# Full-array products in a recurrence, and reordered ends of two expert stages

## The chip, the cores and the metric

One NeuronCore of a Trainium2 chip runs the whole program. The metric is the device time of one execution in microseconds (us), the median of several. The kernel before takes 2805.59 us (three runs, 2804.86 to 2808.12). TensorE does the matrix products, VectorE, ScalarE and GpSimd the elementwise work, and SyncE issues most DMAs. In the rows they are PE (PEld is its weight loads), DVE, ACT, POOL and SP.

## The reference

The reference has two blocks over 1024 tokens of width 1024, all in float32. The first block mixes windowed attention, a gated linear recurrence and an RWKV-7 recurrence. The second has two layers, each a mixer followed by a mixture of 64 experts.

Two parts matter here. The RWKV-7 recurrence, with 4 heads of 64, is

```
sa = state @ (-kk_t)
state = state * w_t + sa * b_t + v_t * k_t      # per head, 64 x 64
y_t = state @ r_t
```

The experts and the end of the network are

```
hh = silu(xb @ w_gate[e]) * (xb @ w_up[e]);  ys = hh @ w_down[e]
h = h + gate_0 * ys_0 + gate_1 * ys_1            # two experts per token
out = rmsnorm(h, final_norm_g)                   # after the last layer
```

## The kernel before

`chunks` computes the recurrence in chunks of 64 tokens, 16 in all. Each chunk needs the inverse of a unit triangular 64 x 64 matrix per head. Four heads lie in two tiles `t` of two 64-row halves. The helper `all_of` issues four 64 x 64 products, one for each tile and half, and these go to the four quarters of the array. Two chunks are in work at once, an even one (`e`) and an odd one (`o`), in the buffers `X[c]` and `Y[c]` of PSUM. The order on every engine is written out by hand in the loops over `ROUNDS`, 8 rounds of two chunks. `cross` begins a chunk with five calls of `all_of`, thus 20 products. `step(J, n)`, for n of 0 to 3, squares the matrix power, multiplies the inverse by it, and adds the old inverse with `all_of(..., eye, ...)`, a product with the 64 x 64 identity `idh`. ScalarE copies each result out (`step_copy`) before the next step may start.

`experts` runs 32 pairs of experts in each layer. SP streams gate, up and down weights into a ring of three slots. For pair `p` PE does the gate products, then `last_product(p - 1)` (the down products of the pair before), the up products, the transposes of the next pair's rows and of the hidden values. POOL gathers rows and scatters results to `ys` in DRAM. After the scatter of the last but one pair it executes a `drain`, and then issues the last scatter. `after.start` loads what the next stage needs, and `after.rows_in` loads rows of `ys` once both scatters' semaphores are in.

After layer 0 the next stage is `combine_and_latents` (class `LatentLoads`), after layer 1 it is `combine_out` (class `FinalLoads`). For each 128-token tile `combine_out` forms the sum of the residual and two gated rows in two VectorE instructions (`gathered_sum`, lines 3554 and 3555), ScalarE squares it, and VectorE scales it (3987, 3988) before SP stores it.

Of the kernel before, what the change touches and what calls it, by code (L numbers as in the profile page):

```python
# [8 lines left out]
ALU = mybir.AluOpType  # L9
# [137 lines left out]
def front(nc, D, proj, values, kkb, bb, dlt, wc, vec, win, ck):  # L147
# [5 lines left out]
    with Phase(nc, "fr") as ph:  # L153
# [73 lines left out]
        with nc.Block() as block:  # L227
# [365 lines left out]
            def _(dve):  # L593
# [160 lines left out]
                V.tensor_tensor(rr, rr, aa[:], ALU.mult)  # L754
                V.scalar_tensor_tensor(out=kkb[:], in0=kkb[:], scalar=-1.0, in1=lw[:], op0=ALU.mult, op1=ALU.mult)
# [190 lines left out]
def chunks(nc, D, proj, kkb, bb, bonus, wc, vec, ck, next_loads):  # L946
# [13 lines left out]
    with Phase(nc, "rwc") as ph:  # L960
        z, masks, idh = ck.z, ck.masks, ck.idh
# [25 lines left out]
        eps_set = ph.sem("eps_set")  # L987

# [16 lines left out]
        with nc.Block() as block:  # L1005
# [49 lines left out]
            def _(dve):  # L1055
                V = nc.vector
                V.memset(eps[:], GN_EPS).then_inc(eps_set, 1)

# [34 lines left out]
                def rows_add(J):  # L1093
                    c, j = place(J)
                    if 0 <= J < NCH:
                        V.tensor_tensor(gr[:, c, :, 1], blocks(Y[c], 1), proj[:, R_T:R_T + TL, columns(J)], ALU.add
                                        ).then_inc(gr_out[c], 1)
# [136 lines left out]
            def _(pe):  # L1234
# [10 lines left out]

                def cross(J):
                    c, j = place(J)
                    if J < NCH:
                        if j:
                            pe.wait_ge(y_out[c], j)  # L1250
                        r, k = (proj[:, f:f + TL, columns(J)] for f in (R_T, CK_T))
                        a, b = (x[:, :, columns(J)] for x in (kkb, bb))
                        all_of(blocks(X[c], 0), b, r, 0, 1)
                        all_of(blocks(X[c], 1), b, a, 0, 1)
                        all_of(blocks(X[c], 2), k, r, 0, 1)
                        all_of(blocks(X[c], 3), k, a, 0, 1)
                        all_of(blocks(X[c], 4), a, b, 0, 1).then_inc(crossed[c], 1)

                def turn_in(J):
                    c, j = place(J)  # L1260
                    if J < NCH:
                        if j:
                            pe.wait_ge(z_out[c], j)
                        val, k = (proj[:, f:f + TL, columns(J)] for f in (CV_T, CK_T))
                        a, b = (x[:, :, columns(J)] for x in (kkb, bb))
# [27 lines left out]
                def step(J, n):  # L1293
                    c, j = place(J)
                    if 0 <= J < NCH:
# [5 lines left out]
                        if n < SQ - 2:  # L1301
                            all_of(blocks(X[c], 1, 2), pw0, flat(steps[:, c, :, 1:3]), at, 1, True, False)
                            all_of(blocks(X[c], 2), eye, steps[:, c, :, 2], at, 1, False, True)
                            last = all_of(blocks(X[c], 0), pw1, pw0, at, 1)
                        elif n == SQ - 2:
                            all_of(blocks(X[c], 1), pw0, steps[:, c, :, 2], at, 1, True, False)
                            all_of(blocks(X[c], 1), eye, steps[:, c, :, 2], at, 1, False, True)
# [43 lines left out]

                for i in range(ROUNDS + 1):
# [419 lines left out]
def first(nc, D, proj, next_loads):  # L1772

    with Phase(nc, "V") as pv:
# [11 lines left out]
        chunks(nc, D, proj, kkb, bb, bonus, wc, vec, ck, next_loads)  # L1786
# [1325 lines left out]
def expert_loads(nc, D, layer):  # L3112
# [12 lines left out]
    return gate_in, up_in, down  # L3125


def experts(nc, D, layer, tokens, keep, spill, gate, gu_slots, d_slots, xe, g_loaded, u_loaded, d_loaded, x_loaded, after, within):
# [4 lines left out]
    gate_in, up_in, down = expert_loads(nc, D, layer)  # L3133
    with Phase(nc, "ex", within) as ph:
# [39 lines left out]
        y_stored = [ph.sem(f"y{b}_stored") for b in range(2)]  # L3174
        hn_dram, y_rows = D["hn"], D["ys"].rearrange("t (c d) -> (t c) d", c=2)
# [150 lines left out]
        with nc.Block() as block:  # L3326

            @block.sync
            def _(sp):
                for p in range(RING, PAIRS_M):  # L3330
# [8 lines left out]
                    for n in range(2):  # L3339
                        down(sp, d_slots[r][n], p + n * PAIRS_M, d_loaded[r])  # L3340
# [4 lines left out]
                after.start(sp)  # L3345
                with sp.If(0 < count):
# [14 lines left out]
                for t in range(after.NBUF):  # L3361
                    after.rows_in(sp, t)

            @block.gpsimd
            def _(pool):
# [23 lines left out]
                for p in range(PAIRS_M - 2, PAIRS_M):  # L3389
                    pool.wait_ge(m["y_out"], 2 * (p + 1))  # L3390
                    scatter(p)
                    if p < PAIRS_M - 1:
                        pool.drain()
                for b in range(2):
# [15 lines left out]
            def _(pe):  # L3410
# [29 lines left out]
                last_product(PAIRS_M - 1)  # L3440
# [23 lines left out]
            def _(act):  # L3464
# [12 lines left out]
                for p in range(PAIRS_M):  # L3477
                    act.wait_ge(m["g_done"], p + 1)
                    silu(p % 2).then_inc(m["silu_done"], 1)
                    if p >= 1:  # L3480
# [26 lines left out]
            def _(dve):  # L3507
# [41 lines left out]
                after.scale_second(nc, dve)  # L3549
# [649 lines left out]
```

## Time and profile before

| | |
|---|---|
| median of three runs | 2805.59 us |
| the profiled execution's own time | 2810.32 us |
| its span | 2808.6 us |
| PE, share of the span | 2464.8 us, 88% |
| DVE | 1072.5 us, 38% |
| ACT | 538.4 us, 19% |
| POOL | 343.6 us, 12% |
| mean granted TensorE clock | 0.95 of full |

The span is the time from the first to the last instruction of the profiled execution. Busy shares are averages over all stages, and each stage has its own limit. The recurrence lies from 384 to 517 us, layer 0's experts end near 1610 us, layer 1's near 2761 us, and `combine_out` runs from there to the end.

### The profile page before, as it was taken

Reading aid. Unit: us, or ns where it says so; the run is one execution under the profiler, and the core shown is the slowest. Engines: PE = TensorE matmul, PEld = TensorE weight load, DVE = VectorE, ACT = ScalarE, POOL = GpSimd, SP = SyncE. Lnnn points to the kernel's source line nnn. Section 1 sums busy time; section 2 is a strip of 40 time slices with the busy share of each in tenths; the row PEclk is TensorE's granted clock in tenths of the full one; section 3 lists DMA queues with packets and bytes.
Section 4 is the critical chain, followed back from the end, with each engine's and each line's share of the span. In section 5 each row is a group of like instructions: output and inputs, shape, how many; then the busy total and the mean of one; then the engine's idle time right before and its main releaser. Section 6 shows DMA issues by size and latency. Waiting matters only on the chain. (4 is left out here: it accounts for less than half of the span.)

```text
span 2808.6 us, 40012 instructions
## 1 busy us (share of the span) xinstructions
PE 2464.8 (88%) x16506; PEld 1581.8 (56%) x16506; DVE 1072.5 (38%) x2183; ACT 538.4 (19%) x1220; POOL 343.6 (12%) x362
## 2 busy tenths in 40 slices
PE   9999988898999898988878789999999988877882
PEld 5444567547888555555545455666674555544551
DVE  3472654666455643211111154444545521111114
ACT  1311454210000011111111131322331111111112
POOL 3321002400000211111111000000004011111110
PEclk9999999998999999999999989999999999999896
DMA  3111010231113237999999970000103499999997
GB/s 116 36 40 53 1 47 5 78 112 37 40 45 117 98 105 280 409 420 419 420 420 420 375 284 16 17 24 8 61 35 144 175 387 419 420 420 420 420 420 300
DMA packets 111033, 566.11 MB, mean 202 GB/s; under 512 B 22000, under 2 KB 22160, under 8 KB 59376
## 3 DMA queue, kind: packets, MB, share of 16 engines
q1 hardware_dynamic: 85808, 506.87, 44.9%
q0 software_dynamic: 20144, 38.79, 3.7%
q10 hardware_dynamic: 4896, 17.83, 1.6%
q8 instruction: 135, 2.21, 0.3%
q14 instruction: 50, 0.41, 0.0%
HBM read 529.06 MB, written 65.01 MB: 212 GB/s over the span
## 5 line engine op out<-in xcount | busy, mean ns | idle before, releaser
L3205 PE MATMUL ex__h_ps<-all__arena,ex__xT 128*64 128x256 f32 x3392 | 529.9, 418 | 166.5 <-DMA all__arena<-in_w_gate 105.6
L3205 PEld LDWEIGHTS ex__h_ps<-all__arena,ex__xT 128*64 128x64 f32 x3392 | 339.6, 151 | 336.4 <-issue 221.5
L3248 DVE COPY ex__ysb<-ex__y_ps 128x512 f32<-128x512 f32 x64 | 44.3, 692 | 630.6 <-PE ex__y_ps L3225 630.2
L3205 PE MATMUL ex__h_ps<-mo__wx,ex__xT 128*64 128x256 f32 x704 | 180.3, 415 | 0.0
L3369 POOL DMA_INDIRECT b__rows<-s_hn,mo__queue x60 | 60.6, 1010 | 760.5 <-PE ex__x_ps L3198 760.5
L3225 PE MATMUL ex__y_ps<-b__w,ex__hT 128*64 128x512 f32 x672 | 152.2, 592 | 0.9 <-ACT ex__hT L3242 0.9
L2535 PE MATMUL cm__acc<-all__arena,cw__w 128*128 128x260 f32 x576 | 136.0, 386 | 2.3 <-PEq L84 2.3
L2535 PE MATMUL cm__acc<-all__arena,cm__sums 128*128 128x260 f32 x576 | 135.0, 384 | 0.0
L2535 PEld LDWEIGHTS cm__acc<-all__arena,cw__w 128*128 128x128 f32 x576 | 110.4, 192 | 19.8 <-issue 2.7
L2535 PEld LDWEIGHTS cm__acc<-all__arena,cm__sums 128*128 128x128 f32 x576 | 110.2, 191 | 17.2
L2921 PE MATMUL hd__o<-all__arena 128*128 128x128 f32 x704 | 98.4, 283 | 15.3 <-ACT all__arena L2990 15.3
L3236 ACT ACTIVATE ex__sg<-ex__h_ps 128x256 f32<-128x256 f32 x64 | 24.5, 383 | 419.3 <-PE ex__h_ps L3205 419.3
L2921 PEld LDWEIGHTS hd__o<-all__arena 128*128 128x128 f32 x704 | 85.5, 191 | 31.9 <-ACT all__arena L2990 25.5
L3205 PEld LDWEIGHTS ex__h_ps<-mo__wx,ex__xT 128*64 128x64 f32 x704 | 103.5, 150 | 0.0
L3239 DVE TENSOR_TENSOR ex__hs<-ex__sg,ex__h_ps 128x256 f32<-128x256 f32 x64 | 27.0, 421 | 186.6 <-PE ex__h_ps L3205 186.6
L3225 PEld LDWEIGHTS ex__y_ps<-b__w,ex__hT 128*64 128x64 f32 x672 | 54.0, 137 | 73.2 <-issue 67.5
L1956 POOL MEMSET mo__ident<- 128x128 f32 x2 | 0.4, 204 | 743.5 <-POOLq L84 743.5
L3230 ACT COPY ex__xT<-ex__x_ps 128x512 f32<-128x512 f32 x64 | 37.4, 585 | 275.6 <-PE ex__x_ps L3198 275.6
L2076 PE MATMUL pb__acc<-b__w,all__arena 128*128 128x512 f32 x192 | 87.9, 603 | 1.8 <-PEq L84 1.8
L374 PE MATMUL fr__acc<-X__xT,fr__w 128*128 128x512 f32 x192 | 87.0, 603 | 0.0
L3198 PE MATMUL ex__x_ps<-mo__ident,b__rows 128*128 128x128 f32 x512 | 75.7, 292 | 9.1 <-PEq L84 9.1
L3198 PEld LDWEIGHTS ex__x_ps<-mo__ident,b__rows 128*128 128x128 f32 x512 | 63.2, 195 | 34.5 <-issue 34.5
(534 smaller groups left out, 4194.9 us busy)
## 6 DMA issues: line engine op xcount, KB each, us to landing
all__arena<-in_w_gate SPq DMA_DIRECT2D x106, 1024.0 KB, 27.7
all__arena<-in_w_up SPq DMA_DIRECT2D x106, 1024.0 KB, 27.1
b__w<-in_w_down SPq DMA_DIRECT2D x84, 1024.0 KB, 27.4
all__arena<-in_w_down SPq DMA_DIRECT2D x22, 1024.0 KB
mo__wx<-in_w_gate SPq DMA_DIRECT2D x22, 1024.0 KB, 28.5
mo__wx<-in_w_up SPq DMA_DIRECT2D x22, 1024.0 KB
mo__wx<-in_w_down SPq DMA_DIRECT2D x22, 1024.0 KB
all__arena<-s_ys SPq DMA_DIRECT2D x16, 1024.0 KB, 8.9
```

Of the source, the lines that this page charges most:

```text
L374: last = mm(acc[:, bank], weight[:, k], moving(k), start=(first and k == 0), stop=(k == HKT - 1), skip_group_check=not first)
L2076: last = mm(acc[:, bank], weight[:, k], moving[:, k], start=(first and k == 0), stop=(last_here and k == HK - 1), skip_group_check=not first)
L2535: last = nc.tensor.matmul(bank(u, x), weight(k), moving(k, c), start=(k == 0), stop=(k == HK - 1))
L2921: last = mm(o_ps[:, h, 0:P], vv[:, s, h], pT[:, h, 4 * g + a], start=(g == 0 and a == 0), stop=(g == end and a == len(tiles_of(i)[g]) - 1))
L3198: last = nc.tensor.transpose(x_ps[:, k // 4, P * (k % 4):P * (k % 4) + P], xe[:, b, k::KT], ident[:])
L3205: last = nc.tensor.matmul(h_ps[half, c, DE * b:DE * b + DE], xT[:, b, k, half], slots[n][:, c, k], start=(k == 0), stop=(k == KT - 1))
L3225: last = nc.tensor.matmul(y_ps[half, c], hT[:, b, k, half], slots[n][:, k, 512 * c:512 * c + 512], start=(k == 0), stop=(k == 1))
L3230: return nc.scalar.copy(xT[:, b, 0:4].rearrange("p k q -> p (k q)"), x_ps[:, 0])
L3236: return nc.scalar.activation(sg[:, b], h_ps[:, 0, DE * b:DE * b + DE], ACT.Silu)
L3239: return nc.vector.tensor_tensor(hs[:, b], sg[:, b], h_ps[:, 1, DE * b:DE * b + DE], ALU.mult)
L3248: return nc.vector.tensor_copy(ysb[:, b, 512:], y_ps[:, 1])
L3369: g.indirect_dma_start(xe[:, p % 2], None, hn_dram[:, :], bass.IndirectOffsetOnAxis(ap=queue[:, 0, p:p + 1], axis=0), bounds_check=T - 1, ...
```

## The change

The changes in the recurrence are these. `front` now leaves `rr` in the tile `XB_T` and `-kk` in `R_T`, so that both are neighbours and one moving operand of 128 columns. `cross` then takes two calls of 128 columns and one of 64, thus 12 products. A new tile `swap` holds the identity with its halves exchanged. `kept` adds the old inverse by two products of the full 128 x 128 array, with `ident` and `swap` as weights, in place of four quarter products.

In `experts`, at the last pair, PE does `last_product(p - 1)` ahead of the gate products, and ACT its half of the copy ahead of `silu`. The last pair's down weights come in four loads, one for each row `k` and expert, with semaphores `d_ends`, and `down_half` computes in the order of `k`. A semaphore `scatter_sent` lets SP issue `after.middle`. `LatentLoads` loads `wk` there, and its residual tiles 1 and 2 between the rows of `ys`. `scale_second` moves from the experts' end into `combine_and_latents`, after `make(1)`. `FinalLoads` loads three residual tiles at first, two in `middle`, three later.

`combine_out` no longer reuses buffers: all eight tiles of rows have their own. For tiles 2, 4 and 6 PE forms the sum, with weights `ident` and `spread` (the identity times a gate's column, made by ACT), and ScalarE and VectorE read it from PSUM. The tiles are taken in the order of `TURNS`.

```diff
-                V.tensor_tensor(rr, rr, aa[:], ALU.mult)
-                V.scalar_tensor_tensor(out=kkb[:], in0=kkb[:], scalar=-1.0, in1=lw[:], op0=ALU.mult, op1=ALU.mult)
+                v(V.tensor_tensor(proj[:, XB_T:XB_T + TL], rr, aa[:], ALU.mult))
+                V.scalar_tensor_tensor(out=rr, in0=kkb[:], scalar=-1.0, in1=lw[:], op0=ALU.mult, op1=ALU.mult)
...
+                V.tensor_copy(swap[:, 0:HALF], ident[:, HALF:P]).then_inc(swap_made, 1)
+                V.tensor_copy(swap[:, HALF:P], ident[:, 0:HALF]).then_inc(swap_made, 1)
...
+                def kept(out, of):
+                    for t, weights in enumerate((ident, swap)):
+                        nc.tensor.matmul(out[:, t], weights[:], of[:, t], start=False, stop=True)
...
-                        r, k = (proj[:, f:f + TL, columns(J)] for f in (R_T, CK_T))
-                        a, b = (x[:, :, columns(J)] for x in (kkb, bb))
-                        all_of(blocks(X[c], 0), b, r, 0, 1)
-                        all_of(blocks(X[c], 1), b, a, 0, 1)
-                        all_of(blocks(X[c], 2), k, r, 0, 1)
-                        all_of(blocks(X[c], 3), k, a, 0, 1)
-                        all_of(blocks(X[c], 4), a, b, 0, 1).then_inc(crossed[c], 1)
+                        ra = proj[:, XB_T:R_T + TL, columns(J)].rearrange("p (f t) k -> p t f k", f=2)
+                        k, b = proj[:, CK_T:CK_T + TL, columns(J)], bb[:, :, columns(J)]
+                        all_of(X[c][:, :, 0:2 * HALF].rearrange("p t (f k) -> p t f k", f=2), b, ra, 0, 1)
+                        all_of(X[c][:, :, 2 * HALF:4 * HALF].rearrange("p t (f k) -> p t f k", f=2), k, ra, 0, 1)
+                        all_of(blocks(X[c], 4), ra[:, :, 1], b, 0, 1).then_inc(crossed[c], 1)
...
                             all_of(blocks(X[c], 1, 2), pw0, flat(steps[:, c, :, 1:3]), at, 1, True, False)
-                            all_of(blocks(X[c], 2), eye, steps[:, c, :, 2], at, 1, False, True)
+                            kept(blocks(X[c], 2), steps[:, c, :, 2])
...
+            return last
+
+        def down_half(b, slots, k):
+            for c in range(2):
+                for n in range(2):
+                    half = slice(CAP * n, CAP * n + CAP)
+                    last = nc.tensor.matmul(y_ps[half, c], hT[:, b, k, half], slots[n][:, k, 512 * c:512 * c + 512],
+                                            start=(k == 0), stop=(k == 1))
...
+                    if p < PAIRS_M - 1:
+                        for n in range(2):
+                            down(sp, d_slots[r][n], p + n * PAIRS_M, d_loaded[r])
+                    else:
+                        for k in range(2):
+                            for n in range(2):
+                                down_rows(sp, d_slots[r][n], p + n * PAIRS_M, k, d_ends[k])
...
                 after.start(sp)
+                sp.wait_ge(scatter_sent, 1)
+                after.middle(sp)
...
+                    end = p == PAIRS_M - 1
+                    if end:
+                        last_product(p - 1)
                     pe.wait_ge(m["xT_out"], 2 * (p + 1))
                     pe.wait_ge(g_loaded[p % RING], 32 * (p // RING + 1))
                     gate_products(p % 2, gu_slots[p % RING]).then_inc(m["g_done"], 1)
-                    if p >= 1:
+                    if p >= 1 and not end:
                         last_product(p - 1)
...
-                last_product(PAIRS_M - 1)
+                pe.wait_ge(m["hT_out"], PAIRS_M)
+                pe.wait_ge(m["y_out"], 2 * (PAIRS_M - 1))
+                for k in range(2):
+                    pe.wait_ge(d_ends[k], 32)
+                    last = down_half((PAIRS_M - 1) % 2, d_slots[(PAIRS_M - 1) % RING], k)
+                last.then_inc(m["y_done"], 1)
...
+    def middle(self, sp):
+        sp.dma_start(self.wk[:], self.D["w_dkv_t"]).then_inc(self.wk_loaded, 16)
+
+    def rows(self, sp):
+        for t in range(self.NBUF):
+            self.rows_in(sp, t)
+            if t + 1 < self.NBUF:
+                self.residual_in(sp, t + 1)
...
                 make(1)
+                pre.scale_second(nc, dve)
                 scale(1)
...
+        BY_PE = (2, 4, 6)
+        TURNS = (0, 1, 3, 2, 5, 4, 7, 6)
...
+                for t in range(NBUF, TT):
+                    if t > NBUF:
+                        pre.residual_in(sp, t)
+                    sp.dma_start(yb[t], D["ys"][P * t:P * t + P]).then_inc(y_loaded[t], 16)
...
+                        nc.tensor.matmul(acc[:, n, c], ident[:], hb[:, t, part_of], start=True, stop=False)
+                        for e in range(2):
+                            last = nc.tensor.matmul(acc[:, n, c], spread[:, n, e], yb[t][:, DM * e + 512 * c:DM * e + 512 * c + 512],
+                                                    start=False, stop=(e == 1))
...
+                make(0)
+                make(1)
+                scale(0)
+                make(3)
+                scale(1)
+                make(5)
+                scale(2)
+                scale(3)
+                make(7)
+                scale(4)
+                scale(5)
+                scale(6)
+                scale(7)
```

On PE, here is a piece of the recurrence's first round: before, from the odd chunk's `cross` to the even chunk's step 0 and the odd chunk's `square`.

```order
L1241 MATMUL rwc__x<-all__arena,V__bb 64x64 x4
L1241 MATMUL rwc__x<-V__kkb,V__bb 64x64 x4
L1241 MATMUL rwc__x<-all__arena 64x64 x4
L1241 MATMUL rwc__x<-V__kkb,all__arena 64x64 x4
L1241 MATMUL rwc__x<-V__bb,V__kkb 64x64 x4
L1241 MATMUL rwc__y<-rwc__big 64x64 x4
L1241 MATMUL rwc__x<-rwc__steps 64x128 x4
L1241 MATMUL rwc__x<-rwc__steps,V__idh 64x64 x4
L1241 MATMUL rwc__x<-rwc__steps 64x64 x4
L1241 MATMUL rwc__x<-rwc__big 64x64 x8
```

The same place on PE now:

```order
L1245 MATMUL rwc__x<-all__arena,V__bb 64x128 x4
L1245 MATMUL rwc__x<-all__arena 64x128 x4
L1245 MATMUL rwc__x<-V__bb,all__arena 64x64 x4
L1245 MATMUL rwc__y<-rwc__big 64x64 x4
L1245 MATMUL rwc__x<-rwc__steps 64x128 x4
L1253 MATMUL rwc__x<-rwc__steps,V__ident 128x64
L1253 MATMUL rwc__x<-rwc__steps,rwc__swap 128x64
L1245 MATMUL rwc__x<-rwc__steps 64x64 x4
L1245 MATMUL rwc__x<-rwc__big 64x64 x8
```

The 20 products of `cross` became 12, and the four quarter products with `idh` became two of the full array, with quarter products on either side of them. A row's shape is that of its output.

On SP, here are the loads at layer 1's end before, from the last pair's gate weights on (`ys` rows are those of the final stage):

```order
L3117 DMA all__arena<-in_w_gate 128x2048
L3117 DMA mo__wx<-in_w_gate 128x2048
L3120 DMA all__arena<-in_w_up 128x2048
L3120 DMA mo__wx<-in_w_up 128x2048
L3123 DMA b__w<-in_w_down 128x2048 x2
L3923 DMA all__arena<-s_h 128x1024 x8
L3924 DMA all__arena<-in_final_norm_g 128x1024
...
L3933 DMA all__arena<-s_ys 128x2048 x4
...
L3933 DMA all__arena<-s_ys 128x2048
L3960 DMA out<-all__arena 128x1024
L3933 DMA all__arena<-s_ys 128x2048
```

And now:

```order
L3125 DMA all__arena<-in_w_gate 128x2048
L3125 DMA mo__wx<-in_w_gate 128x2048
L3128 DMA all__arena<-in_w_up 128x2048
L3128 DMA mo__wx<-in_w_up 128x2048
L3134 DMA b__w<-in_w_down 128x1024 x4
L3972 DMA all__arena<-in_final_norm_g 128x1024
L3985 DMA all__arena<-s_h 128x1024 x5
...
L3991 DMA all__arena<-s_ys 128x2048 x4
...
L4028 DMA all__arena<-s_ys 128x2048
L3985 DMA all__arena<-s_h 128x1024
L4028 DMA all__arena<-s_ys 128x2048
```

Three residual loads moved behind the first five tiles of rows, and the stores of `out` moved behind all loads.

## Rows read from the trace of the kernel before

**Rows 1.** The chain of waits, layer 1's end: start us, us, what.

```profile
2714.22 28.23 DMA mo__wx<-in_w_gate
...
2742.59 3.67 PE ex__h_ps L3205 x32
2746.26 3.45 PE ex__y_ps L3225 x16
...
2752.24 8.47 issue
...
2761.46 4.05 DMA s_ys<-ex__ysb,mo__queue
...
2765.96 7.31 DMA all__arena<-s_ys
...
2773.37 1.30 DVE all__arena L3554
...
2802.65 1.29 DVE all__arena L3988
```

**Rows 2.** Groups of instructions, DVE, 2770 to 2808 us: count, busy us, mean ns.

```profile
L3555 DVE SCALAR_TENSOR_TENSOR all__arena<-all__arena,all__gate 128x1024 f32<-128x1024 f32 x8 | 10.3, 1285 | 0.3
L3988 DVE SCALAR_TENSOR_TENSOR all__arena<-all__arena,co__rs 128x1024 f32<-128x1024 f32 x8 | 10.3, 1285 | 0.3
...
L3987 DVE RECIPROCAL co__rs<-co__rt 128x1 f32<-128x1 f32 x8 | 1.3, 163 | 1.0
```

**Rows 3.** Busy time by stretch, line 1241: length, PE, PEld (counts), clock, DMA.

```profile
384.00:517.00 133.00, 109.51 (x4322) 98.69 (x4323) 0.98 0.08 28
```

**Rows 4.** DMA queues, 384 to 517 us: packets, MB, share of 16 engines.

```profile
q8 instruction: 34, 0.56, 1.8%
```

**Rows 5.** Waits, 384 to 517 us: who for whom, us in total, times, longest.

```profile
PE rwc__x L1241 <- issue: 14.6, 19, 1.8
...
PE rwc__y L1241 <- issue: 3.3, 5, 0.9
...
PEld rwc__x L1241 <- ACT rwc__steps L1181: 5.9, 21, 0.7
```

**Rows 6.** Timeline of PE, 434 to 453 us: start, us, [idle before].

```profile
443.60 0.21 PE L1241 MATMUL rwc__y<-V__idh,all__arena 64*64 64x64 f32 x1 [0.81 <-issue]
```

**Rows 7.** Timeline of PE, 441.2 to 442.3 us.

```profile
441.31 0.45 PE L1241 MATMUL rwc__x<-rwc__steps 64*64 64x128 f32 x8
441.58 0.29 PE L1241 MATMUL rwc__x<-rwc__steps,V__idh 64*64 64x64 f32 x8
...
442.03 0.29 PE L1241 MATMUL rwc__x<-rwc__steps,V__idh 64*64 64x64 f32 x8
442.14 0.30 PE L1241 MATMUL rwc__x<-rwc__steps 64*64 64x64 f32 x8
```

**Rows 8.** Timeline of PE's weight loads, 441 us, quarter array.

```profile
441.31 0.21 PEld L1241 LDWEIGHTS rwc__x<-rwc__steps 64*64 64x64 f32 x8 [0.29 <-ACT rwc__steps L1181]
```

**Rows 9.** Timelines of PE, 300 us, and PEld, 2739 us: changes of the array's tiling.

```profile
300.10 1.02 PE L838 MATMUL swa__f<-X__xT,all__arena 128*128 128x512 f32 x2
301.05 0.72 PE L804 MATMUL swa__s<-all__arena 64*128 64x128 f32 x8
...
2739.27 0.97 PEld L3198 LDWEIGHTS ex__x_ps<-mo__ident,b__rows 128*128 128x128 f32 x8 [0.39 <-issue]
```

**Rows 10.** Timelines of POOL, PE and DVE, layer 0's end.

```profile
1613.00 0.97 POOL L3374 DMA_INDIRECT s_ys<-ex__ysb,mo__queue  x1 [9.86 <-issue]
...
1592.01 0.66 PE L3205 MATMUL ex__h_ps<-all__arena,ex__xT 128*64 128x256 f32 x1 [4.24 <-DMA mo__wx<-in_w_gate]
...
1610.07 2.46 DVE L3600 TENSOR_SCALAR all__arena<-all__arena,fw__gains 128x320 f32<-128x320 f32 x8
1621.30 1.28 DVE L3554 SCALAR_TENSOR_TENSOR all__arena<-all__arena,all__gate 128x1024 f32<-128x1024 f32 x1 [8.78 <-DMA all__arena<-s_ys]
```

**Rows 11.** Busy time by stretch: length, PE, PEld, DVE, ACT, POOL, clock, DMA share, GB/s.

```profile
1580.00:1590.00 10.00, 7.77 (x56) 4.83 (x52) 1.80 (x3) 1.45 (x3) 0.97 (x1) 1.00 1.01 420
```

More of the change, by code:

```diff
@@ L1263, in turn_in @@
                             pe.wait_ge(z_out[c], j)
[L1264 to L1265 removed]
+                        a, val, k = (proj[:, f:f + TL, columns(J)] for f in (R_T, CV_T, CK_T))
+                        b = bb[:, :, columns(J)]
                         all_of(blocks(Y[c], 0), a, eye, 0, 1)
@@ L1306, in step @@
                             all_of(blocks(X[c], 1), pw0, steps[:, c, :, 2], at, 1, True, False)
-                            all_of(blocks(X[c], 1), eye, steps[:, c, :, 2], at, 1, False, True)
+                            kept(blocks(X[c], 1), steps[:, c, :, 2])
                             last = all_of(blocks(X[c], 0), pw1, pw0, at, 1)
@@ L3174, in experts @@
         y_stored = [ph.sem(f"y{b}_stored") for b in range(2)]
+        d_ends = [ph.sem(f"d_end{k}_loaded") for k in range(2)]
+        scatter_sent = ph.sem("scatter_sent")
         hn_dram, y_rows = D["hn"], D["ys"].rearrange("t (c d) -> (t c) d", c=2)
@@ L3360, in _ @@
                     sp.wait_ge(y_stored[b], 16 * (PAIRS_M // 2))
-                for t in range(after.NBUF):
-                    after.rows_in(sp, t)
+                after.rows(sp)
             @block.gpsimd
@@ L3477, in _ @@
                 for p in range(PAIRS_M):
+                    end = p == PAIRS_M - 1
+                    if end:
+                        y_half(p - 1)
                     act.wait_ge(m["g_done"], p + 1)
                     silu(p % 2).then_inc(m["silu_done"], 1)
-                    if p >= 1:
+                    if p >= 1 and not end:
                         y_half(p - 1)
@@ L3921, in start, with middle, rows, residual_in @@
     def start(self, sp):
-        for t in range(self.TT):
-            sp.dma_start(self.hb[:, t], self.h_in[P * t:P * t + P]).then_inc(self.h_loaded[t], 16)
         sp.dma_start(self.gb[:], self.D["final_norm_g_2"].partition_broadcast(P)).then_inc(self.g_loaded, 16)
+        for t in range(3):
+            self.residual_in(sp, t)
+    def middle(self, sp):
+        for t in range(3, 5):
+            self.residual_in(sp, t)
+    def rows(self, sp):
+        for t in range(self.NBUF):
+            self.rows_in(sp, t)
+    def residual_in(self, sp, t):
+        sp.dma_start(self.hb[:, t], self.h_in[P * t:P * t + P]).then_inc(self.h_loaded[t], 16)
     def scale_first(self, nc, act):
-        pass
-    def scale_second(self, nc, dve):
         pass
@@ new lines, in _ @@
+                for n, t in enumerate(TURNS):
+                    sp.wait_ge(scaled, n + 1)
+                    sp.dma_start(D["out"][P * t:P * t + P], ho[:, t]).then_inc(out_stored, 16)
+                sp.wait_ge(out_stored, 16 * TT)
+            @block.gpsimd
+            def _(pool):
+                make_identity(nc, pool, ident, const_done)
+                nc.gpsimd.memset(eps[:], NORM_EPS).then_inc(const_done, 1)
+            @block.tensor
+            def _(pe):
+                pe.wait_ge(const_done, 3)
+                for n, t in enumerate(BY_PE):
+                    pe.wait_ge(h_loaded[t], 16)
+                    pe.wait_ge(spread_done, 2 * (n + 1))
+                    pe.wait_ge(y_loaded[t], 16)
+                    for c in range(2):
+                        part_of = slice(512 * c, 512 * c + 512)
+                        nc.tensor.matmul(acc[:, n, c], ident[:], hb[:, t, part_of], start=True, stop=False)
+                        for e in range(2):
+                            last = nc.tensor.matmul(acc[:, n, c], spread[:, n, e], yb[t][:, DM * e + 512 * c:DM * e + 512 * c + 512],
+                                                    start=False, stop=(e == 1))
+                    last.then_inc(summed, 1)
@@ new lines, in _ @@
+                for n, t in enumerate(BY_PE):
+                    for e in range(2):
+                        nc.scalar.activation(spread[:, n, e], ident[:], ACT.Copy, scale=gate[:, t, e:e + 1]
+                                             ).then_inc(spread_done, 1)
+                nc.scalar.activation(rt[:, 1:2], eps[:], ACT.Sqrt)
+                for n, t in enumerate(TURNS):
+                    b = n % 2
+                    if t in BY_PE:
+                        act.wait_ge(summed, BY_PE.index(t) + 1)
+                    else:
+                        act.wait_ge(made, by_dve.index(t) + 1)
+                    if n >= 2:
+                        act.wait_ge(scaled, n - 1)
+                    nc.scalar.activation(sq[:], sums_of(t), ACT.Square, accum_out=ss[:, b:b + 1]).then_inc(squared, 1)
+                    act.wait_ge(squared, n + 1)
@@ L4049, in moe @@
         x_loaded = [ph.sem(f"x{b}_loaded") for b in range(2)]
-        gate_in, up_in, down = expert_loads(nc, D, layer)
+        gate_in, up_in, down, _ = expert_loads(nc, D, layer)
         gu = lambda tile: part(tile, 2, KT, DE)
```

92 lines of the change are left out of this document (42 added, 50 removed).

## The prediction

> **What bounds the kernel now.** I read the chain of waits first, then the stretches it passes through. At layer 1's end it shows a row of single causes [rows 1]: the last gate weights land at 2742.45 us, PE does gate products and then the down products of the pair before, GpSimd sits 8.47 us between its last two scatters, the last scatter lands, the first rows of `ys` land, and from there VectorE alone carries the chain to 2803.94. Layer 0 ends the same way [rows 10].
>
> The recurrence is 133 us in which PE is busy for 109.5 and DMA is nearly idle [rows 3]. The reader should look at the queue of instructions there: 34 packets with 0.56 MB, thus 16 KB each [rows 4]. `chunks` issues 136 products for each of 16 chunks, and every one appears as two weight loads and two matmuls, 8704 instructions in all (8645 are recorded, rows 3). 8704 over 34 packets is 256, so a packet is 256 instructions. PE's idle time has mostly no releaser, "issue": 14.6 and 3.3 us [rows 5], in gaps like the one of 0.81 us [rows 6]. 133 us over 34 packets is 3.9 us a packet. I read this as PE waiting for its own instructions: it uses up 256 in about 3 us and gets the next after 3.9. After these come short waits for ScalarE's copy of a step, 5.9 us [rows 5].
>
> **The recurrence, removed and added.** Four quarter products run side by side. With 64 columns they take 0.115 us (442.03 to 442.14 [rows 7]); with 128 columns 0.27 us after a wait, of which some 0.05 are the first weights, so 0.22 [rows 7].
>
> `cross`: five calls at 0.115 are 0.575 us; now twice 0.22 and once 0.115 are 0.555. That gains 0.02 x 16 = 0.3 us of PE, but 8 products, thus 32 instructions, a chunk. `kept` saves two products, 8 instructions, in each of four steps, 32 more. 64 x 16 = 1024 instructions are four packets. Were the stage bound by packets alone, it would take 30 x 3.9 = 117 us.
>
> The price of `kept` stands in no row, so I build it. Its weights are 128 columns wide. Eight such loads in a row take 0.97 us, 0.11 from one to the next [rows 9], against about 0.055 for a round of quarter loads (two rounds in 0.21, one lasting 0.13 [rows 8]). Two products need four loads, and only 64 columns stream behind each, half as long as its successor's load. That is 4 x 0.11 + 0.055 = 0.495 us. Second, the array's tiling changes before and after. In rows 9 two full-array matmuls start 0.43 apart, so the second starts at 300.53 and has streamed by 300.96; the first of the other tiling starts at 301.05. That is 0.09 us in which nothing streams, and the first weight load behind it is open too (counted above going in, 0.055 going out). Together 0.09 + 0.495 + 0.09 + 0.055 = 0.73 us, in place of 0.115: 0.61 us more. Four steps in 16 chunks are 64 calls, 39 us of PE.
>
> The Trainium skill, "TensorEngine Tiling (Array Packing)", section Tiling Modes, Key Properties, says that changing the tiling mode, not merely the tile, drains TensorE. By that rule the 0.09 us are paid twice in every call, as the trace has it between other stages; without it 64 x 0.18 = 11.5 us would fall away and the kernel would come out near 2797 us, which is inside the first rival below.
>
> What hides it: the instruction waits. PE without them needs some 133 - 22 = 111 us (17.9 in rows 5, and a few us in gaps of the weight loads, which I set at 4). Plus 39, less 0.3: 150. In the steps PE alternates between two chunks. With 0.61 more for each, ScalarE's copies are always ready, so their 5.9 us go: 144. A block that now has fewer slow steps will still meet its packet late, 2 us. So 146 us, **+13 us**. The packets (117) are then no longer late on the whole. Bounds: -16 (packets alone decide, `kept` is free) and +28 (all 39 is added, and only 11 of the waits go). I take 13, since each of its terms has a row. Nothing covers the stage: all later stages start after it. The two copies for `swap` (VectorE, 128 x 64) and the moved outputs of `front` cost under 0.5 us.
>
> **Layer 0's end.** PE waits 4.24 us for gate weights until 1592.01 [rows 10]. The down products (3.45 us, as rows 1) now fit into this gap, from about 1588.5. But the up weights, 2.1 MB at 420 GB/s [rows 11], land 5 us after the gate ones, near 1597, so the up products start 3.5 us earlier than before and not more. The hidden copy and down products follow, and the last down weights (another 5 us, 1602) are just there. So the last results leave PE 3.5 us earlier. GpSimd's scatter at 1613.00 was late through its drain (9.86 us idle); the scatter before it moves ahead by over 8 us, so the drain is over, and the last scatter follows its data by 0.8 us in place of 2.9. Gain 5.6 us. Against it: `wk` (1.3 MB, 3.1 us) is now in the queue ahead of the rows and beside the scatter. I take off 1.1. The eight `scale_second` instructions (2.46 us) now stand on VectorE after `make(1)`, where it waited about 2 us for ScalarE; PE is the engine behind and has work. **-4.5 us**, bounds -5.6 and -1.
>
> **Layer 1's end.** PE waited only 1.9 us for the gate weights, so the down products move ahead, but products in all end 1.0 us earlier. The drain again: 1.6 us. The last scatter 2.6 us earlier; two residual loads (1 MB) now run beside it, which I price at 0.4. `combine_out`: before, VectorE takes 33.4 us, from 2770.5 (one sum and its wait ahead of 2773.37) to 2803.94, eight times two sums of 1.28, a reciprocal and a scaling of 1.285 and gaps [rows 1, 2]. Three tiles' sums leave it: 25 us of work. But then the loads bound it: after the first rows, 7 tiles of 1.05 MB and 3 residuals of 0.52 are 8.9 MB, 21.2 us at 420 GB/s; tile 7's sum and four scalings (2.6 + 4 x 1.5 with PSUM sources) end at 29.8. Gain 3.6. PE's six products for a tile are 12 matmuls at 0.43 [rows 9], 5.2 us at 2.4 GHz and 10.3 at 1.2 GHz; after idling it starts slowly (the first gate matmul of rows 10 lasts 0.66 us). Tile 6 is ready in time at the higher and 1 us late at the lower. **-5.8 us**, bounds -8 and -2.
>
> **Sum.** 13 - 4.5 - 5.8 = +2.7 us. Against its own time (span 2808.6, 2810.32 us in all) the profiled execution would become 2813.0. The median of the runs lies 4.7 below that, so 2805.6 + 2.7 = 2808 us. A measurement of this kernel tells differences over about 0.2%, 5.6 us; this is none.
>
> **Rivals.**
> Cheap full-array products: the loads are pulled ahead or the drain overlaps, and the packets decide. For it: PE idles 22 us today, and 1024 instructions go. Against: the gap of 0.09 and the 0.11 between loads. Stage 117 to 135 us, kernel 2779 to 2797, say 2789.
> Dear ones (slower): the stalls for packets do not give way, since where steps are dense the packets were not late and elsewhere they still are. It decides once more than 30 of the 39 us remain; then +23 in the stage, 2818 us. For it: the gap of rows 6 lies in a run of products that read no step. Against: there is a packet every 3.9 us, and each 256 instructions now hold two `kept`.
> The ends give nothing: the scatter is held by the new loads and rows land no earlier, or the final stage stays as long through PE at 1.2 GHz. Half of the gain: 2813 us. Against: the drain's 8.47 us in the chain.
>
> **Chances.** Forecast 0.48 (its own range 2801 to 2814), cheap 0.28, dear 0.16, ends 0.08. Faster by over 0.2%: 0.28 + 0.48 x 0.12 = 0.34. Slower: 0.16 + 0.06 and 0.15 of the forecast's 0.48 = 0.29. The same: 0.37. The range 2785 to 2819 leaves out the ends of both outer cases.
>
> **What would show it.** In the profile after: the recurrence at 146 us with 30 packets, "issue" on PE under 8 us, and about 0.6 us between the starts of the first full-array product and the next quarter product. A stretch of 120 us would refute the price of `kept`. GpSimd's last scatter 0.8 us behind VectorE's copy at both ends, and VectorE waiting for `ys` of tile 7. If the stage's idle time stayed at 18 us with `kept` in it, the reading of packets would be wrong.

## The result, and the profile after

The changed kernel takes 2818.86 us (median of 6 runs, 2815.07 to 2819.79), the kernel before, run beside it, 2806.86 us (2803.83 to 2808.87). The ratio is 1.0034, with a 95% interval of 1.0024 to 1.0044: slower by 9.5 us, 6.7 to 12.3. The two medians by themselves lie 12.0 us apart and the two profiled executions 8.9; this text goes by the ratio. The forecast was +2.7 us, 2808, and its own range ended at 2814. The range over all cases, 2785 to 2819, just holds the 2818.86, but only through the rival "dear ones" (2818), and the mechanism of that rival is not the one that acted. That the number lies there is luck.

A time is only the sum. What to read is when each stage begins in the two profiled executions (spans 2808.6 and 2817.5 us); the difference can only grow or shrink where something was changed, or where two executions of the same code differ. These are worked out from the records of each stage's tiles ("gate weights" is the start of the pair's first gate product; the recurrence is counted from the start of its first to the start of its last instruction):

| point in the program | before | after | difference |
|---|---|---|---|
| recurrence: first to last instruction | 137.6 | 149.4 | +11.8 |
| layer 0, experts begin | 1110.8 | 1121.5 | +10.7 |
| layer 0, gate weights of the pair before the two last | 1558.8 | 1570.3 | +11.5 |
| layer 0, last copy of results | 1609.37 | 1617.55 | +8.2 |
| layer 0, last scatter issued | 1613.00 | 1619.04 | +6.0 |
| layer 0, it has landed, rows of `ys` issued | 1615.98 | 1625.43 | +9.5 |
| attention's head stage begins | 1731.2 | 1741.8 | +10.6 |
| layer 1, gate weights, middle of the stream | 2512.4 | 2522.9 | +10.6 |
| layer 1, last copy of results | 2758.47 | 2769.56 | +11.1 |
| layer 1, last scatter issued | 2761.46 | 2771.04 | +9.6 |
| layer 1, landed, rows issued | 2765.59 | 2776.97 | +11.4 |
| first sum of the final stage | 2770.53 | 2782.40 | +11.9 |
| last scaling ends | 2803.9 | 2812.9 | +9.0 |

**The recurrence.** First what answers to [rows 3]: length of the window, busy us (and count) of PE, PEld, DVE, ACT and POOL, then the granted clock, DMA's share and GB/s.

```profile
384.00:532.00 148.00, 140.68 (x3840) 121.90 (x3840) 57.06 (x228) 65.86 (x177) 27.03 (x61) 0.98 0.07 25
```

PE now is busy for 140.7 of 148 us, where it was for 109.5 of 133. The instruction queue in the same stretch, answering to [rows 4]:

```profile
q8 instruction: 30, 0.49, 1.3%
```

And the waits of PE and of its weight loads, answering to [rows 5]: for what, us in total, times, the longest.

```profile
PE rwc__x L1245 <- ACT rwc__steps L1185: 3.0, 8, 0.4
PE rwc__y L1245 <- DVE rwc__yn L1138: 2.3, 2, 1.8
PEld rwc__x L1253 <- issue: 8.4, 48, 0.4
```

"issue" is gone from PE's matmuls. The 8.4 us on the weight loads of line 1253 are inside the full-array products. One such call (timeline of PE; a float32 product shows as two matmuls): six of the eight matmuls of four quarter products, which run side by side, then the two full-array products, then quarter products again.

```profile
459.69 0.39 PE L1245 MATMUL rwc__x<-rwc__steps 64*64 64x128 f32 x6
460.01 0.43 PE L1253 MATMUL rwc__x<-rwc__steps,V__ident 128*128 128x64 f32 x2
460.28 0.39 PE L1253 MATMUL rwc__x<-rwc__steps,rwc__swap 128*128 128x64 f32 x2
460.59 0.34 PE L1245 MATMUL rwc__x<-rwc__steps 64*64 64x64 f32 x8
```

In the records behind these rows the last quarter matmul starts at 459.81 and the next one behind the call at 460.59, 0.79 us later. In 48 of the 64 calls it is 0.79, made of 0.20, 0.16, twice 0.112, and 0.205 (in the other 16 it is 0.74); less the 0.056 that lie between two matmuls anyway, a call takes 0.73 us, the price that the prediction built.

**Layer 0's end.** VectorE, GpSimd and the DMA issues in after (start, us, what ended the idle time before), answering to [rows 10]:

```profile
1617.55 0.69 DVE L3269 COPY ex__ysb<-ex__y_ps 128x512 f32<-128x512 f32 x1 [4.79 <-PE ex__y_ps L3246]
1630.81 1.28 DVE L3592 SCALAR_TENSOR_TENSOR all__arena<-all__arena,all__gate 128x1024 f32<-128x1024 f32 x1 [12.57 <-DMA all__arena<-s_ys]
```
```profile
1619.04 0.98 POOL L3401 DMA_INDIRECT s_ys<-ex__ysb,mo__queue  x1 [11.16 <-DVE ex__ysb L3269]
```
```profile
1618.85 0.33 SPq L3626 DMA_DIRECT2D all__arena<-in_w_dkv_t  x1
1625.43 0.33 SPq L3654 DMA_DIRECT2D all__arena<-s_ys  x1
```

The reader should see three things. The last scatter now waits for VectorE's copy and follows its end by 0.8 us; the drain is no longer in the way. But by these records SP issues the load of `wk` 0.2 us ahead of it: `sem_inc` stands behind the scatter in the program and yet counted before the scatter's recorded start. And the rows of `ys` leave 6.4 us after the scatter, where before it was 3.0. What the DMA queues moved in the two halves of that time (q1 carries SP's loads, q0 the scatter; packets, MB, share of 16 engines), first from 1619 to 1622 us, then from 1622 to 1625.5:

```profile
q1 hardware_dynamic: 64, 0.66, 69.4%
```
```profile
q1 hardware_dynamic: 80, 0.66, 51.3%
q0 software_dynamic: 144, 0.30, 22.1%
```

The 1.3 MB of `wk` go first. In the first half not one packet of the scatter ends; all 144 are in the second. By the single DMA records its first packet starts at 1623.84, when 1.12 of the 1.31 MB have moved. Small as it is, 0.3 MB, it stands behind nearly the whole load.

**Layer 1's end.** PE's gate products of pair 30, before and after (timeline of PE):

```profile
2727.09 5.36 PE L3205 MATMUL ex__h_ps<-all__arena,ex__xT 128*64 128x256 f32 x32 [3.10 <-DMA all__arena<-in_w_gate]
```
```profile
2738.11 6.63 PE L3218 MATMUL ex__h_ps<-all__arena,ex__xT 128*64 128x256 f32 x32 [5.22 <-DMA all__arena<-in_w_gate]
```

It had idled for 5.2 in place of 3.1 us, and the same 32 products took 1.3 us more; the granted clock was lower around them, 0.57 against 0.76, so more of them ran at 1.2 GHz, the lower of the clock's two levels. These are the windows of before and of after, with the clock third from the end:

```profile
2726.00:2733.00 7.00, 5.91 (x36) 4.18 (x38) 0.00 (x0) 0.38 (x1) 0.00 (x0) 0.76 1.01 423
```
```profile
2737.00:2745.00 8.00, 6.88 (x35) 4.32 (x37) 0.00 (x0) 0.22 (x1) 0.00 (x0) 0.57 1.01 421
```

From there PE's work is the limit. The 1.0 us that the reordered down products save is thus lost before it begins. Nothing that PE does ahead of pair 31 was changed, and the idle time before the gate products of pairs 27 to 30 goes 1.9, 4.3, 3.1, 3.1 us in before and 3.1, 4.3, 2.0, 5.2 in after. As far as these records show, this loss is one of the two executions, not of the change. Then GpSimd and SP:

```profile
2758.91 0.98 POOL L3401 DMA_INDIRECT s_ys<-ex__ysb,mo__queue  x1 [8.17 <-DVE ex__ysb L3269]
2771.04 0.98 POOL L3401 DMA_INDIRECT s_ys<-ex__ysb,mo__queue  x1 [11.16 <-DVE ex__ysb L3269]
```
```profile
2745.13 26.53 SPq L3985 DMA_DIRECT2D all__arena<-s_h  x5
2776.97 1.98 SPq L3991 DMA_DIRECT2D all__arena<-s_ys  x4
```

Again 0.8 us from the copy to the scatter, and 5.9 us from there to the rows, where it was 4.1. The 4.1 were themselves unusual: of nine profiled executions with this end unchanged, seven show 3.0 us here and one other 4.1. Of the two residual loads one left 0.2 us ahead of the scatter, the other 0.2 us behind it. These are the last pieces of the chain of waits in after, answering to the end of [rows 1]:

```profile
2782.94 21.14 DMA co__own_rows<-s_ys
2804.18 1.30 DVE co__ho L3592
2805.50 1.30 DVE co__ho L3593
...
2811.61 1.28 DVE co__ho L4090
```

The final stage has become a stream of loads: tile 7 lands 21.1 us after its issue and 21.8 us after the first rows (2782.26 to 2804.08), for which the prediction had 21.2. From the first sum to the last scaling it takes 30.5 us, 33.4 before.

### The profile page after: what moved, and what is told of

It reads as the page before. It is cut to its first block and busy times, and to the rows that moved or that the text cites. A ratio compares the mean times of both kernels' runs of the same rounds, so it can differ in the third digit from the quotient of the medians.

```text
span 2817.5 us, 39067 instructions
## 1 busy us (share of the span) xinstructions
PE 2513.5 (89%) x16030; PEld 1607.7 (57%) x16030; DVE 1065.5 (38%) x2178; ACT 541.1 (19%) x1226; POOL 345.8 (12%) x365
## 5 line engine op out<-in xcount | busy, mean ns | idle before, releaser
L3238 PE MATMUL ex__y_ps<-b__w,ex__hT 128*64 128x512 f32 x640 | 144.8, 592 | 0.0
## 6 DMA issues: line engine op xcount, KB each, us to landing
all__arena<-in_w_gate SPq DMA_DIRECT2D x106, 1024.0 KB, 27.8
all__arena<-in_w_down SPq DMA_DIRECT2D x22, 1024.0 KB, 27.4
```

## Experiments

Each ran on a chip beside the kernel before; a difference is (ratio - 1) x that median, with its interval. "Stage" is the recurrence from its first to its last instruction. A first thing the runs show: four profiled executions with the same recurrence as before had stages of 137.6, 135.1, 136.1 and 134.4 us, 135.8 in the mean. The one on which the prediction rests was the longest.

**The two halves of the change.** Recurrence alone (`front`, `chunks` as in the change, the rest as before):

> The kernel before with the recurrence's part of the change alone (12 products in cross, the old inverse by full-array products), both experts' ends and the final stage as before. Theory A: the recurrence costs what it costs in the changed kernel (137.6 -> 149.4 us from its first to its last instruction), and the ends gave back only 2 us of it: the kernel is 11 us slower than before (9 to 13). Rival B (the ends themselves gained about what was forecast, and the recurrence costs more than its own stage shows): 16 us or more slower.

Measured: +14.3 us (10.4 to 18.3), median 2823.53; stage 150.1 us, 14.3 over the mean of before. The ends alone:

> The kernel before with the experts' ends and the final stage of the change alone, the recurrence as before. Theory A: 2 us faster (0 to 4), since in both layers the last scatter leaves 2 to 5 us earlier but lands 2 to 3.4 us later, beside the loads now sent with it. Rival B, the forecast: 10 us faster.

Measured: -2.0 us (-4.5 to +0.6), median 2807.69. B is refuted in its half on the ends: they give a fifth of what was forecast. For the recurrence alone A's 11 (9 to 13) was too low and B wanted 16 or more; the interval holds both. The stage's own 14.3 us are the whole 14.3, so nothing is lost outside it, and A's mechanism holds: A had measured from the longest stage of before. The cost is near the +13 of the forecast. The last scatters took 6.6 and 6.3 us to land.

**The two parts of the recurrence.** Twelve products, but in each step

```
-                            kept(blocks(X[c], 2), steps[:, c, :, 2])
+                            all_of(blocks(X[c], 2), eye, steps[:, c, :, 2], at, 1, False, True)
```

> The kernel before with 12 products in place of 20 in cross, the old inverse still added by quarter products. TensorE's own work changes by 0.3 us, but 512 of its instructions go, 2 of 34 packets. Theory A (before is bound by the arrival of instruction packets, 3.9 us each): the recurrence is 8 us shorter (6 to 12), the kernel as much faster. Rival C (the waits in before have another cause): within 1 us of before.

Measured: -5.6 us (-8.1 to -2.8), stage 129.9 us, 5.9 under the mean; the last run below, with the same recurrence, has 129.8. C is excluded; A has the sign, and its 8 (6 to 12) was a little too much. The other way round, `kept` with the twenty products:

> The kernel before with the old inverse added by two full-array products in each step, cross with its 20 products. 64 calls at 0.61 us are 39 us of TensorE more, and 2 packets fewer. Theory A (either the packets or the work is late, and here the work is): about 12 us slower in the recurrence (11 to 15), thus like the run with both parts of the recurrence. Rival D (the waits for packets stay and the work is added to them): 16 to 25 us slower.

Measured: +19.1 us (15.2 to 23.0), stage 153.3 us, 17.5 over the mean. A's 11 to 15 are missed, and both figures lie in D's 16 to 25. But D's mechanism is not there. The packets and the waits that nothing releases, of this run:

```profile
q8 instruction: 32, 0.52, 1.3%
```
```profile
PE rwc__x L1245 <- issue: 1.1, 3, 0.5
PE rwc__y L1245 <- issue: 0.5, 1, 0.5
```

The waits did give way (14.6 and 3.3 us in [rows 5]). What A lacked was in part the mean: it reckoned 22 us of waits in a stage that is 2 us shorter on average. The number alone would have misled, as it does for the whole change.

**What a call of `kept` is made of.** Behind its two products two more, with zero weights:

```
+                    for t in range(2):
+                        nc.tensor.matmul(out[:, t], nought[:], of[:, t], start=False, stop=True)
```

> The kernel before with the recurrence's part of the change, and in each of the 64 calls two more full-array products, whose weights are zero and which add nothing. They stand behind the first two, so the array's tiling changes no more often. Theory A (two full-array products are four weight loads of 0.11 to 0.13 us each, the rest of a call's 0.73 us is the change of tiling before and after): 28 to 33 us slower than the run with the recurrence alone. Rival F (most of a call's price is the change of tiling, and more products behind it cost 0.055 us each): 7 us slower.

Measured: +44.6 us (40.4 to 49.1), so 30 more than the recurrence alone; 30 / 64 is 0.47 us for two products, and in the records 0.83 us lie between the first and last matmul of a call in place of 0.38. Theory A, and F's 7 us is refuted: two products cost 0.45 us, four loads of 0.112. Of 0.73 us the remaining 0.28 go with the two changes of tiling, 0.14 each in the mean. This is a remainder; no run changed the tiling without the products.

**Are the gaps the packets'?** I counted matmuls from the start of the stage to each place where two starts lie over 0.28 us apart and PE waited for no semaphore. In before the first are at 267, 395, 522, 649, 775, 903, 1156, 1282, 1410, that is 267 and steps of 127 matmuls, each with its weight load: 254 instructions and one or two waits, 256. There are 27 such gaps, all on this grid, with 22.8 us above the usual 0.056. With 12 products there are 21 gaps and 14.0 us; with `kept` alone 8 and 3.5; in the run with the whole recurrence part 3 and 1.0. The DMA records say the same from the other side: in before, PE resumes 1.20 to 1.57 us after the end of an instruction packet at every one of the 27 gaps, while only 8% of all its matmuls start in that distance from a packet. The packets start 3.3 to 4.5 us apart there, 3.8 in the mean. So the gaps are waits for packets. To weigh the packets by a test I added instructions. First semaphore counts, 8 behind each of four steps:

```
+                        if n < SQ - 1:
+                            for _ in range(8):
+                                pe.sem_inc(counted, 1)
```

> The kernel before with 32 instructions more for TensorE in each of 16 chunks (8 behind each of four steps), which only add one to a semaphore that nobody reads: 512 instructions, two packets, as many as one of the recurrence's two parts takes away. Theory A (a packet of 256 instructions comes every 3.9 us, and before waits for it): the recurrence is 8 us longer in the sum, plus what these instructions cost by themselves, which the next run shows. Rival C (the gaps have another cause): longer only by what the next run shows.

> The kernel before with the recurrence's part of the change and the same 512 instructions. Here TensorE needs 149 us for its work and the packets would come in 32 x 3.9 = 125 us, so they are early. Theory A: longer than the recurrence alone only by what the instructions cost by themselves, 0 to 5 us, and at least 5 us less than they cost in the last run. Rival C: the same cost in both.

Measured: +42 us (37 to 47) and +26 us (21 to 30); stages 179.5 and 163.4 us. So the same 512 counts cost 43.7 us over the mean of before and 13.3 us over the recurrence alone. The sign is A's, the size of neither theory, and as a weighing of packets this test failed. A count is not cheap: they stand 0.15 us apart in the records, so eight keep PE's queue for 1.2 us. And in the first of the two runs the clock fell, which it did not in the second (columns as in after's window above; two windows of the first run, then one of the second):

```profile
386.00:470.00 84.00, 63.02 (x2053) 57.22 (x2047) 24.67 (x92) 31.13 (x81) 10.70 (x25) 0.83 0.11 40
470.00:560.00 90.00, 70.79 (x2247) 64.72 (x2243) 30.78 (x123) 34.27 (x96) 14.99 (x34) 0.79 0.01 4
```
```profile
386.00:470.00 84.00, 80.83 (x2052) 68.45 (x2044) 29.32 (x112) 34.99 (x92) 13.69 (x31) 0.98 0.11 39
```

The second attempt added narrow products in `cross`:

```
+                        for _ in range(4):
+                            all_of(X[c][:, :, 7 * HALF:7 * HALF + 8], b, b[:, :, 0:8], 0, 1)
```

> The kernel before with 16 more quarter products in each of 16 chunks (4 rounds of 4, only 8 columns wide, into a part of PSUM that nobody reads): 1024 instructions for TensorE, 4 packets, as many as the change takes away. By themselves they take at most what 64-column rounds take, 0.115 us each, so up to 7 us in all; the next run shows it. Theory A (a packet every 3.9 us, and before waits for it): the recurrence 12 to 20 us longer. Rival C (the gaps have another cause): as much longer as in the next run, up to 7 us.

> The kernel before with the recurrence's part of the change and the same 1024 instructions. It then needs 34 packets, 133 us, and TensorE has 149 us of work. Theory A: longer than the recurrence alone by the products' own time, 3 to 8 us, and by 7 us or more less than in the last run. Rival C: the same cost in both.

Measured: +14.6 us (9.5 to 19.4) and +27.8 us (23 to 32.6); stages 148.5 and 159.4 us. By the stages they cost 12.7 us over the mean of before, and 9.3 us over the recurrence alone, where packets are early; by the times 14.6 and 13.5 us, which are closer still. One gap of the first run, and its packets:

```profile
457.63 0.27 PE L1241 MATMUL rwc__x<-V__kkb,all__arena 64*64 64x64 f32 x2 [0.80 <-issue]
```
```profile
q8 instruction: 38, 0.62, 1.7%
```

Here the gaps are on nearly the same grid (267, 395, 649, 777, 903, 1031, ...) though other instructions stand there, all 30 of them end 1.2 to 1.5 us after a packet's end, and 38 packets by 3.9 us are 148.2. But the products' own price was 0.145 us a round, over my 0.115, and the two costs differ by 3 us by the stages and 1 us by the times, where A wanted 7 and C none; a stage varies by 3 us from one execution to the next. So this pair does not tell A from C. That the gaps are waits for packets is shown by the records. How much shorter the stage would be with all of them early is not: 12 products took 2 packets and 6 us, with 0.03 us a chunk of own work.

**What holds the last scatter up.** The ends again, but with `wk` and the two residual tiles issued in `start`, behind the last weights:

```
-                sp.wait_ge(scatter_sent, 1)
-                after.middle(sp)
```

> The run with the ends alone, but the loads that were issued between the last scatter and the rows of `ys` (wk in layer 0, two residual tiles in layer 1) are issued before it, behind the last weights, as in the kernel before. Theory A (these loads hold the last scatter up: it landed 6.4 us after its issue in layer 0 in place of 3.0, 5.9 in place of 4.1 in layer 1): both last scatters land in 3 to 4.2 us again; 5 us faster than the run with the ends alone, about 7 us faster than before. Rival E (the landing is longer for another reason, such as the rows of the scatter before it, which now leave closer to it): the landings stay at 6 us, no gain over the ends alone.

Measured: -9.8 us (-13.5 to -6.5), median 2797.58, and the two landings 3.0 and 3.5 us. GpSimd and SP in layer 0:

```profile
1606.23 0.97 POOL L3390 DMA_INDIRECT s_ys<-ex__ysb,mo__queue  x1 [11.34 <-DVE ex__ysb L3260]
```
```profile
1609.22 0.33 SPq L3640 DMA_DIRECT2D all__arena<-s_ys  x1
```

E is refuted: the scatter before the last stands as close as in the ends alone (12.3 and 12.4 us), only the load beside it is gone. In time the ends now give what the prediction gave them, 9.8 for 10.3, and more than A's 7; in the traces 2.7 us from layer 0's first expert to the head stage and 5.1 from layer 1's first expert to the last scaling. With the ends unchanged these two stretches themselves vary by 2 us between four executions (619.1 to 621.3 and 542.5 to 544.5 us). One step further:

```
-                pre.scale_second(nc, dve)
+                after.scale_second(nc, dve)
...
-        for t in range(5):
+        for t in range(self.TT):
             self.residual_in(sp, t)
```

> As the last, and moreover the eight scalings of wk stand in the experts' end again, and all eight residual tiles of layer 1 are loaded before its last scatter, so that the rows of `ys` are alone in the queue behind it. Expected: 1 us from the scalings, since VectorE no longer does 2.46 us of them between the second and third tile; and 2 to 3 us from the final stage, whose last tile waits for 1.5 MB less (3.7 us at 420 GB/s). In all 3 us faster than the last, 10 us faster than before (6 to 12). Rival: the residual tiles delay the last scatter or the last weights by as much, no gain.

Measured: -9.8 us (-13.2 to -6.5), median 2796.95, no gain over the last. In layer 1, GpSimd, SP and VectorE:

```profile
2753.30 0.97 POOL L3390 DMA_INDIRECT s_ys<-ex__ysb,mo__queue  x1 [12.33 <-DVE ex__ysb L3260]
```
```profile
2759.80 1.96 SPq L3976 DMA_DIRECT2D all__arena<-s_ys  x4
```
```profile
2764.65 1.29 DVE L3581 SCALAR_TENSOR_TENSOR co__ho<-all__arena,all__gate 128x1024 f32<-128x1024 f32 x1 [12.13 <-DMA all__arena<-s_ys]
```

The final stage did become 3.4 us shorter (27.4 us from the first sum to the last scaling, 30.8 in the run before). But the residual tiles were still under way when the scatter left, and its rows of `ys` were issued 6.5 us after it, where it was 3.5: 3.0 given back. The rival was right, by the same mechanism. The 1 us expected from the scalings does not show in the time either. Last, these ends with the twelve products and without full-array products:

> The ends of the last run with the recurrence of 12 products in cross and the old inverse by quarter products. If the parts add up: 10 us for the ends and 5.6 us for the 12 products, 15 us faster than before (11 to 18).

Measured: -14.0 us (-18.0 to -10.1), median 2792.65 (2790.06 to 2795.02), expected 15 (11 to 18). The parts add up, and this version beats both kernels.

## Why the prediction was right, and where its terms were wrong

The measured time lies at the very end of the range, and the forecast itself, +2.7 us, missed by 7. One of its three terms held. The other two, the ends of the layers, were wrong in the same step: what a load costs that is issued together with the last scatter.

**Recurrence, +13 us: right.** Measured +11.8 us between the two profiled stages and +14.3 us by the run with it alone. The 146 us were reckoned from the window 384 to 517, which ends before the stage does; counted as in the table above, the stage went from 137.6 to 149.4. The price of `kept` (0.73 us) was right to the hundredth, from 0.11 a load and 0.09 and 0.055 at each change of tiling, thus 0.44 and 0.29; the added products put the split at 0.45 and 0.28. "Issue" on PE's matmuls is near 0, and 30 packets came. The Trainium skill, "TensorEngine Tiling (Array Packing)", section Tiling Modes, Key Properties, says that changing the mode drains the array. The run with the doubled products agrees that a change costs time, 0.14 us; that it is a drain, no run here shows. The cheap rival (0.28) is refuted by the stage, the dear one (0.16) by the waits that went, though its 2818 us is where the kernel landed. `cross` by itself gained 6 us in a stage that waits for packets. Beside full-array products it gained 3.2 us (153.3 less 150.1), of which 2.5 are gaps; its own work is 0.03 us a chunk less.

**Layer 0's end, -4.5 us: wrong, about 0 to -1.** The steps up to the scatter held. The last copy came 3.3 us earlier against the stream (11.5 less 8.2; forecast 3.5) and the last scatter 5.5 (forecast 5.6). The step that failed is "I take off 1.1" for `wk`. It cost 3.4 us, its whole duration (1.3 MB at 420 GB/s, 3.1 us), since the scatter's packets came behind it; with `wk` issued early the landing was 3.0 us again. I took a shared queue to slow a small transfer down in part. The prediction had the 3.1 us in its hand, and [rows 10] had the chain that goes through this landing. Another 1.1 us were lost up to the head stage. The scalings between the second and third tile, called covered, are the suspect; in the two runs that had them back the stretch from the first product of `cl` to the head stage was 105.0 and 105.7 us, 105.6, 105.1 and 105.9 in the three with them there, and 104.1 to 104.5 in the nine with layer 0's end as before. So they are not the cause, or not alone; the new order of residual tiles is another candidate, and this is open.

**Layer 1's end, -5.8 us: wrong, -1.6** (9.0 less 10.6). By terms: the products in all 1.0 earlier in the forecast, 0.5 later here, for PE had the lower clock at pair 30; drain 1.6, measured 1.5; contention 0.4, measured 1.8 at the scatter and 0.5 at the first rows; final stage 3.6, measured 2.9, for the loads took 21.8 us in place of 21.2. The step that failed is again the price of the loads beside the scatter, the 0.4. Against the usual 3.0 us of this landing they cost 2.9 us, more than their own duration (1 MB at 420 GB/s, 2.5 us). Without the two loads beside the scatter this layer gave 5.1 us.

The rival "the ends give nothing" had 0.08 and 2813 us. It was the right one, with its first reason, "the scatter is held by the new loads". I had written against it the drain's 8.47 us in the chain. That was no argument: the drain went, and the transfer behind it grew.

## What to carry to other kernels

A transfer at the end of a chain should have the queues to itself. A load issued at the same moment cost its whole duration here, though the transfer that mattered was small; issue it early enough to have landed, or after the landing. And a semaphore counted behind the scatter in program order did not say that the scatter had been sent: it let the load out first. Whether a load sent just behind the scatter would have cost less was not tried. Where an engine uses its instructions up faster than they arrive, fewer instructions help as such (6 us for 512 of them), but not if each step then pays 0.61 us for wider weight loads and two changes of tiling.

## What the runs showed of the hardware

- A change between quarter and full-array products on PE costs 0.14 us in the mean (what remains of a call's 0.73 us), and two full-array fp32 products 64 columns wide cost 0.45 us, as much as four starts 0.112 us apart.
- PE's instructions come in packets of 16 KB, 256 instructions, 3.3 to 4.5 us apart in a stage that waits for them; all 27 gaps of the stage before lie on the packets' borders and end 1.2 to 1.6 us after a packet.
- A semaphore count on PE takes 0.15 us of its queue; 512 of them made the stage of the kernel before 43.7 us longer, with a granted clock of 0.79 to 0.83 where it is 0.98 otherwise, but the stage with full-array products only 13.3 us, at 0.98 to 1.00.
- The rows that wait for an indirect scatter of 0.3 MB can be issued 3.0 us after it when little else is under way, 3.5 to 4.3 us when a few earlier loads still land, and 5.9 to 6.6 us after it beside loads of 1.0 to 1.3 MB.
